# Seven experts' results through a table in device memory, fetched per token, in place of spreading matmuls

## The reference, cut to what matters

```python
def moe_swiglu(h, w_router, w1, w3, w2):
    logits = (h @ w_router).astype(jnp.float32)
    top_val, top_idx = lax.top_k(logits, TOP_K)          # TOP_K = 2
    probs = jax.nn.softmax(top_val, axis=-1)
    combine = jnp.sum(jax.nn.one_hot(top_idx, N_EXPERTS, dtype=jnp.float32) * probs[..., None], axis=-2)
    combine = combine.astype(h.dtype)
    out = jnp.zeros_like(h)
    for e in range(N_EXPERTS):
        out = out + combine[..., e:e + 1] * swiglu(h, w1[e], w3[e], w2[e])
    return out
```

## Time and profile before

| | us |
|---|---|
| runs, median (lowest to highest) | 2058.24 (2054.41 to 2058.87) |
| the profiled execution's own time | 2054.22 |
| its span, first to last instruction | 2052.4 |
| PE busy | 2012.1 (98%) |
| VectorE busy | 1580.0 (77%) |
| ScalarE busy | 1247.0 (61%) |
| POOL busy | 13.9 (1%) |
| HBM read; written | 513.28 MB; 2.12 MB |

### The profile page before, as it was taken

How to read it: one execution, slowest core, us unless ns; L and a number is a source line. 1 busy time by engine, 2 the same in 40 slices (tenths; PEclk the granted TensorE clock), 3 DMA queues, 4 the chain that set the end, 5 groups by cost and what they waited for, 6 DMA issues and landing times.

```text
span 2052.4 us, 28693 instructions
## 1 busy us (share of the span) xinstructions
PE 2012.1 (98%) x10737; PEld 1722.1 (84%) x10737; DVE 1580.0 (77%) x1218; ACT 1247.0 (61%) x1060; POOL 13.9 (1%) x21
## 2 busy tenths in 40 slices
PE   9999999999999999999989999999999999999998
PEld 8988888789998987888878888888888888888887
DVE  5778855755445878865768898888989889898987
ACT  5655455443334664455447777777777777777775
POOL 0000000000000000000000000000000000000000
PEclk9999999999999999999999999999999999999999
DMA  8523455255554523455249999999999999999996
GB/s 277 167 80 106 143 182 184 83 184 185 184 184 146 183 83 103 144 172 182 98 154 329 378 364 380 370 358 377 358 382 353 380 369 357 377 358 381 354 374 243
DMA packets 240765, 516.53 MB, mean 252 GB/s; under 512 B 11528, under 2 KB 34312, under 8 KB 240686
## 3 DMA queue, kind: packets, MB, share of 16 engines
q1 hardware_dynamic: 238274, 507.33, 69.9%
q0 software_dynamic: 2144, 7.88, 1.1%
q10 hardware_dynamic: 268, 0.22, 0.0%
HBM read 513.28 MB, written 2.12 MB: 251 GB/s over the span
## 4 chain that ended last, share of the span: by engine, by line
PE 92%; DVE 4%; issue 2%; ACT 2%; DVEq 0%; ACTq 0%
PE PS L476 27%; PE PS L478 27%; PE PS L477 27%; PE PS L560 7%; PE PS L1063 1%; ACT hi L1186 1%; PE PS L1026 1%; PE PS L780 1%; PE PS L694 0%; PE PS L811 0%; DVE t_n L1704 0%; PE PS L1014 0%; DVE b_gc L2014 0%; PE PS L493 0%; PE PS L649 0%
## 5 line engine op out<-in xcount | busy, mean ns | idle before, releaser
L1681 DVE TENSOR_TENSOR lo<-raw,hi 128x2048 fp32r<-128x2048 f32 x481 | 1095.8, 2290 | 289.9 <-ACT hi L1186 287.6
L1186 ACT ACTIVATE hi<-raw 128x2048 fp32r<-128x2048 f32 x481 | 919.7, 1915 | 314.1 <-PE PS L478 307.9
L476 PE MATMUL PS<-hi,e_hi 128*128 128x512 f32 x896 | 355.1, 396 | 1.4 <-DVE e_lo L1704 1.4
L478 PE MATMUL PS<-hi,e_lo 128*128 128x512 f32 x896 | 349.5, 390 | 0.0
L477 PE MATMUL PS<-lo,e_hi 128*128 128x512 f32 x896 | 349.0, 389 | 0.0
L476 PE MATMUL PS<-hi,actT_hi 128*128 128x512 f32 x640 | 253.4, 396 | 3.7 <-DVE lo L1681 3.1
L478 PE MATMUL PS<-hi,actT_lo 128*128 128x512 f32 x640 | 249.6, 390 | 0.0
L477 PE MATMUL PS<-lo,actT_hi 128*128 128x512 f32 x640 | 249.2, 389 | 0.0
L476 PE MATMUL PS<-hi,fT_hi 128*128 128x512 f32 x536 | 208.7, 389 | 0.0
L478 PE MATMUL PS<-hi,fT_lo 128*128 128x512 f32 x536 | 208.7, 389 | 0.0
L477 PE MATMUL PS<-lo,fT_hi 128*128 128x512 f32 x536 | 208.6, 389 | 0.0
(11 more groups left out here) (329 smaller groups left out, 2112.0 us busy)
## 6 DMA issues: line engine op xcount, KB each, us to landing
raw<-in_moe_w SPq DMA_DIRECT2D x336, 1024.0 KB, 5.3
raw<-in_w_in SPq DMA_DIRECT2D x92, 1024.0 KB, 5.1
raw<-in_ffn_w SPq DMA_DIRECT2D x33, 1024.0 KB, 5.2
raw<-in_w_br SPq DMA_DIRECT2D x12, 1024.0 KB, 5.0
raw<-in_w_out SPq DMA_DIRECT2D x8, 1024.0 KB, 5.1
bias<-hankel_dram POOLq DMA_DIRECT2D x1, 1536.0 KB, 12.7
x<-in_x SPq DMA_DIRECT2D x2, 512.0 KB, 5.5
f_gain<-in_norm_ffn POOLq DMA_DIRECT2D x2, 512.0 KB, 3.8
```

What stands on the lines that cost most here:

```text
L476: pe.matmul(out, a_hi, b_hi, start=first, stop=False, skip_group_check=True)
L478: return pe.matmul(out, a_lo, b_hi, start=False, stop=last, skip_group_check=True)
L1186: act.activation(hi[prog.u % SPLIT][:, :], raw[slot][:, :], COPY).then_inc(hi_made.sem, 1)
L1681: dve.tensor_tensor(lo[prog.u % RAW][:, :], raw[prog.u % RAW][:, :], hi[s][:, :].bitcast(F32), ALU.subtract).then_inc(lo_made.sem, 1)
```

## The change: what it does

- The result of expert 0 to 6 is copied by ScalarE (`results_out`) to a float32 tile `y_out` (it has to wait until the write before it has landed) and written by POOL to rows n*128 to n*128+127 of a table `y_dram` in device memory (512 KB each). Rows 896 to 1023 are written once with zeros.
- `scatter` (line 1026), `results` on VectorE (`y_lo`), `add_to_x` (line 2235) and the two transposes of `pick` with their copy are left out of the first turn, except for the last expert, which keeps its spreading at the end. TensorE's wait for VectorE's read of x's sum before `down` becomes a wait for `y_hi_made`, the copy of ScalarE.
- VectorE computes once, in expert 0 (`places`), which table row each token's first and second choice stands in (the zero row where the choice is expert 7 or was not held).
- In expert 7, POOL waits until all seven results have landed and then fetches four tiles of 128 rows x 1024 by indirect DMAs (two token tiles by two choices) into `y_back`, 16 KB per partition; VectorE adds each to x with its weight (`add_back`), one in each of steps 3 to 5, for which the loop is written out, and one before `results_last`.

```diff
@@ -265,9 +266,13 @@
     xT = sb("xT", [P, TT, KT, P], at=bias_at)
     y_hi = sb("y_hi", [P, D], F32R, at=bias_at)
     y_lo = sb("y_lo", [P, D], F32R, at=bias_at + 4096)
+    y_out = sb("y_out", [P, D], at=bias_at + 8192)
+    y_back = sb("y_back", [P, 2 * TT, D])
+    y_at = sb("y_at", [P, 2 * TT], U32)
     PS = ctx.enter_context(nc.psum_tensor("PS", [P, 8, 512], F32))
     fn_dram = nc.dram_tensor("fn_dram", (T, D), F32, kind="Internal").ap()
+    y_dram = nc.dram_tensor("y_dram", (E * P, D), F32, kind="Internal").ap()
...
@@ -1018,8 +1022,8 @@
         def scatter(n):
-            pe.wait_ge(pickT_made.sem, n + 1)
-            pe.wait_ge(y_lo_made.sem, y_lo_made.count(n + 1))
+            pe.wait_ge(pickT_made.sem, n - SPREAD + 1)
+            pe.wait_ge(y_lo_made.sem, y_lo_made.count(n - SPREAD + 1))
             for t in range(TT):
                 for half in range(2):
                     for part, src in enumerate((y_hi, y_lo)):
...
@@ -1093,14 +1097,17 @@
                 down(base - 1, last=True)
             turn_f(base)
             up(0)
-            if not first:
+            if turn and not first:
                 scatter(n - 1)
-            for t in range(TT):
-                ins = pe.transpose(PS[:, 3, t * P:(t + 1) * P], pick[:, t, :], ident)
-            ins.then_inc(pickT_done.sem, 1)
+            if turn or last:
+                for t in range(TT):
+                    ins = pe.transpose(PS[:, 3, t * P:(t + 1) * P], pick[:, t, :], ident)
+                ins.then_inc(pickT_done.sem, 1)
             up(1)
-            if not first:
-                pe.wait_ge(s_read.sem, s_read.count(2 * n - 1))
+            if turn and not first:
+                pe.wait_ge(s_read.sem, s_read.count((n - SPREAD) * 2 - 1))
+            elif not first:
+                pe.wait_ge(y_hi_made.sem, n)
             down(base, first=True)
             turn_f(base + 1)
             step(base + 2)
...
@@ -1574,6 +1581,12 @@
             act.wait_ge(unit_used.sem, used)
             act.activation(y_hi[:, :], bank(4, 5), COPY).then_inc(y_hi_made.sem, 1)
+        def results_out(n, used):
+            act.wait_ge(unit_used.sem, used)
+            act.wait_ge(fn_out.sem, n * 16 + 32)
+            act.activation(y_out[:, :], bank(4, 5), COPY).then_inc(y_hi_made.sem, 1)
         def results_last(turn, used):
             act.wait_ge(y_half.sem, turn + 1)
...
@@ -1597,15 +1610,18 @@
             prep(1)
             silu(base, U + 2 if first else U)
             prep(2 if first else 4)
-            if not first:
+            if not first and turn:
                 results(U + 4)
+            elif not first:
+                results_out(n - 1, U + 4)
             high(base)
             prep(1)
             prep(1)
             silu(base + 1, U + 6)
             prep(1)
-            act.wait_ge(pickT_done.sem, pickT_done.count(n + 1))
-            act.activation(flat(pickT), PS[:, 3, 0:T], COPY).then_inc(pickT_made.sem, 1)
+            if turn or last:
+                act.wait_ge(pickT_done.sem, pickT_done.count(n - SPREAD + 1))
+                act.activation(flat(pickT), PS[:, 3, 0:T], COPY).then_inc(pickT_made.sem, 1)
             prep(3)
             high(base + 1)
             prep(1)
...
@@ -2241,13 +2258,38 @@
...
+        def places():
+            dve.wait_ge(slots_here.sem, 6)
+            pos, base, val, part = (r_t[:, n, :] for n in (14, 16, 17, 18))
+            tt(val, pos, base, ALU.add).then_inc(dve_step.sem, 1)
+            dve.wait_ge(dve_step.sem, prog.step())
+            dve.scalar_tensor_tensor(val, pos, float(P), val, ALU.is_lt, ALU.mult).then_inc(dve_step.sem, 1)
+            dve.wait_ge(dve_step.sem, prog.step())
+            for k in range(2):
+                tt(part, r_t[:, 4 + k, :], val, ALU.mult).then_inc(dve_step.sem, 1)
+                dve.wait_ge(dve_step.sem, prog.step())
+                dve.tensor_reduce(r_t[:, 19, k * TT:(k + 1) * TT], part.rearrange("p (t e) -> p t e", t=TT),
+                                  AX.X, ALU.add).then_inc(dve_step.sem, 1)
+                dve.wait_ge(dve_step.sem, prog.step())
+            dve.tensor_scalar(y_at[:, :], r_t[:, 19, 0:2 * TT], float(SPREAD * P), None, ALU.add).then_inc(row_made.sem, 1)
+        def add_back(c):
+            if c == 0:
+                dve.wait_ge(e_rows_here.sem, 16 * (SPREAD + 2 * TT))
+            t = c % TT
+            dve.scalar_tensor_tensor(x[:, t, :], y_back[:, c, :], r_t[:, 11, c:c + 1], x[:, t, :],
+                                     ALU.mult, ALU.add).then_inc(dve_step.sem, 1)
+            dve.wait_ge(dve_step.sem, prog.step())
...
@@ -2276,17 +2318,19 @@
             prep(2 if first else 3)
             multiply(base, U + (4 if first else 2))
             prep(1 if first else 2)
-            if not first:
+            if turn and not first:
                 results(n - 1)
             low(base)
             prep(1)
             prep(1)
-            if not first:
+            if turn and not first:
                 for t in range(TT):
                     add_to_x(n - 1, e - 1, t)
             prep(2)
             multiply(base + 1, U + 8)
             prep(2)
+            if first and turn == 0:
+                places()
             if not last:
                 choose(n + 1, e + 1, turn)
             low(base + 1)
...
@@ -2298,12 +2342,21 @@
             prep(1)
             if not last and turn == 0:
                 keep_row(n + 1)
-            with prog.loop(dve, STEPS_EXPERT - 4, 0) as i:
-                prep(3)
-                multiply(base + 3 + i, i * 6 + (U + 20))
-                prep(2)
-                low(base + 3 + i)
-                prep(1)
+            if last and turn == 0:
+                for i in range(STEPS_EXPERT - 4):
+                    prep(3)
+                    multiply(base + 3 + i, i * 6 + (U + 20))
+                    prep(2)
+                    low(base + 3 + i)
+                    prep(1)
+                    add_back(i)
...
...
@@ -2445,15 +2500,29 @@
         pool.iota(slots_i[:, 0:TT], pattern=[[P, TT]], base=0, channel_multiplier=1).then_inc(slots_here.sem, 1)
         pool.wait_ge(slots_here.sem, 3)
         pool.tensor_copy(ids[:, :], slots_i[:, 0:TT]).then_inc(slots_here.sem, 1)
+        pool.wait_ge(slots_here.sem, 4)
+        pool.iota(slots_i[:, 0:TT * E], pattern=[[0, TT], [P, E]], base=-SPREAD * P, channel_multiplier=0)\
+            .then_inc(slots_here.sem, 1)
+        pool.wait_ge(slots_here.sem, 5)
+        pool.tensor_copy(r_t[:, 16, :], slots_i[:, 0:TT * E]).then_inc(slots_here.sem, 1)
+        pool.memset(y_out[:, :], 0.0).then_inc(slots_here.sem, 1)
         pool.wait_ge(norm_made.sem, norm_made.at(1, 5))
         pool.dma_start(fn_dram.rearrange("(t p) d -> p t d", p=P), fn[:, :, :]).then_inc(fn_out.sem, 16)
         pool.wait_ge(fn_out.sem, 16)
+        pool.wait_ge(slots_here.sem, 7)
+        pool.dma_start(y_dram[SPREAD * P:E * P, :], y_out[:, :]).then_inc(fn_out.sem, 16)
         for n in range(1, E):
-            pool.wait_ge(row_made.sem, n)
+            pool.wait_ge(row_made.sem, n + 1)
             if n > 1:
                 pool.wait_ge(e_done.sem, e_done.count(2 * n))
             pool.indirect_dma_start(e_rows[:, :], None, fn_dram[:, :],
                                     bass.IndirectOffsetOnAxis(ap=row_i[:, 0:1], axis=0)).then_inc(e_rows_here.sem, 16)
+            pool.wait_ge(y_hi_made.sem, n)
+            pool.dma_start(y_dram[(n - 1) * P:n * P, :], y_out[:, :]).then_inc(fn_out.sem, 16)
+        pool.wait_ge(fn_out.sem, 32 + 16 * SPREAD)
+        for c in range(2 * TT):
+            pool.indirect_dma_start(y_back[:, c, :], None, y_dram[:, :],
+                                    bass.IndirectOffsetOnAxis(ap=y_at[:, c:c + 1], axis=0)).then_inc(e_rows_here.sem, 16)
```

More of the change, by code:

```diff
@@ L68 @@
 PAIRS = E // 2
+SPREAD = E - 1
 K_ID, K_LE, K_GT, K_M0, K_MT, K_N = 0, 1, 2, 3, 4, 11
@@ L1002, in find_rows @@
         def find_rows(n):
-            pe.wait_ge(pickT_made.sem, n)
             pe.wait_ge(pick_made.sem, 2 * n + 2)
@@ L1113, in expert @@
             if not last:
-                if not first:
-                    pe.wait_ge(s_read.sem, s_read.count(2 * n))
+                if turn and not first:
+                    pe.wait_ge(s_read.sem, s_read.count((n - SPREAD) * 2))
                 if turn == 0:
@@ L1133, in experts @@
             if turn:
-                pe.wait_ge(s_read.sem, s_read.count(2 * E * turn))
+                pe.wait_ge(s_read.sem, s_read.count(2))
             n = E * turn
@@ L2211, in choose @@
             dve.wait_ge(e_done.sem, e_done.count(2 * n))
-            dve.wait_ge(pickT_done.sem, pickT_done.count(n))
+            if turn:
+                dve.wait_ge(pickT_done.sem, pickT_done.count(n - SPREAD))
             for t in range(TT):
@@ L2231, in add_to_x @@
         def add_to_x(n, e, t):
-            dve.wait_ge(s_done.sem, 2 * n + t + 1)
+            dve.wait_ge(s_done.sem, (n - SPREAD) * 2 + t + 1)
```

(21 more changed lines are left out.)

## The result

The changed kernel took 2068.47 us (median of 5 runs, 2067.58 to 2069.97), beside 2058.24 us before (5 runs, 2054.41 to 2058.87): ratio 1.0055, 95% interval 1.004 to 1.007. It is slower by 10.2 us. The forecast was 2045, faster by 13, with 2038 to 2053 as its range.

A forecast was written before the change was run, and what follows sets the result against it. The prediction took TensorE, busy 98%, as the bound, with weight DMA nearly as tight. Removed work of 14.6 us less 2.2 us for the burst gave -12.4 us, so 2045 us, range 2038 to 2053.

The forecast's parts named there:

- the removal: TensorE: spreading matmuls and `pick` transposes go in seven experts, 14.6 us saved, all on the path.
- Landing: Weight units: land within 9.0 us behind one write, 10.7 to 13.3 us behind the last expert's four gathers.
- `places` in expert 0: VectorE, expert 0: seven small operations, 1.2 us once, covered by slack, so no cost.
- burst of four gathers: Expert 7: four gathers, 2.1 MB, hold up the weights; TensorE idle 2.2 us, bounds 0 and 8.8.
- three add_backs in steps: VectorE, steps 3 to 5 of expert 7: one add_back of about 1.29 us each, at no cost.
- The period: Experts 1 to 6, gather to gather: 119.0 us instead of 121.08, DMA having room at 379 GB/s.
- 9.8 us bound: Weight units: a landing up to 9.8 us after being asked for costs TensorE nothing.
- in front of the weights: DMA queues: POOL's transfers go first, queue 0 having 96.3% and the weights' queue 3.9% while a gather moves.
- 16.4 still fits: VectorE, steps 3 to 5 of expert 7: 15.1 us of work becomes 16.4 with an add_back, within 16.81.
- (d): Rival, slower: weights already at a DMA ceiling of 369 GB/s, experts take 122.3 us, total 2072; chance 0.05.
- (c): Rival, no change, 2058: ceiling a little below 379 GB/s, or TensorE idle at the down's new wait; chance 0.08.
- (b): Rival, dear burst in expert 7: each small transfer costs weights 2.4 us, total 2052.4 or 2048.4; chance 0.14.

The follow-up runs named there:

- after_pad4: Changed kernel with four waits on a signal given long ago put into TensorE's program ahead of its loop over expert pairs: 2049.23 us, ratio 0.9967.
- flat_best: flat_halves, with ScalarE's `hi` copy also put ahead of `y_out` and `places` computed ahead of expert 0: 2045.8 us, ratio 0.9947 to the kernel before.
- flat_halves: flat_spread, with each add_back also cut into two halves of 512 columns at VectorE's gaps: 2047.62 us, ratio 0.996 to the kernel before.
- flat_spread: Changed kernel with TensorE's pair loop written out, the last expert's gathers seven units apart, each add_back waiting for its own: 2046.31 us, ratio 0.9951.

## Why the prediction was wrong

**The step that failed** is the removal: "7 x 1.86 = 13.0 us, 7 x 0.22 = 1.5 us: 14.6 us (...), all of it on the path". As time that is right. The sum has no term for what the removal does to the code, so it stands at nothing, and 21.1 us were measured. I took instructions for time only. They are also code, and TensorE's loop begins behind them. Four fewer ahead of it (the pair of transposes in expert 0, which I had even counted) put its start at -2, and each of the two jumps back then cost 9.64 and 11.46 us. The trace of before had the hint, queue 8, empty in two turns of the loop: something that could be lost.

The account for the profiled execution, against the span of before (the burst is taken from after_pad4, see **Landing**):

| | forecast, us | measured, us |
|---|---|---|
| spreading and transposes gone | -14.6 | -14.6, less 7 x 0.19 = 1.3 |
| `places` in expert 0 | 0 | +0.6 |
| burst of four gathers | +2.2 | +3.0 |
| three add_backs in steps | 0 | +1.5 |
| two misses | not seen | +21.1 |
| already later ahead of the experts | - | +2.1 |
| sum | -12.4 | +15.0 (span: +15.4) |

**The period.** 119.0 forecast, 119.18 measured, at 379 GB/s: DMA had the room. The 0.19 us have a place. ScalarE now copies `y_out` (1.03 us), `fT_hi`, and only then `hi`, so VectorE gets that `hi` late and one step takes 17.04 instead of 16.81 us. The spreading matmuls had covered it; I had named the order but priced it at nothing. flat_best turned the order round and its periods grew, so that part is argued and not shown.

**places**: two blocks of transposes of expert 0 are 34.47 us apart. Before it was 34.09, less the 0.22 of the transposes 33.87, so 0.6 us are new. I had called it covered.

**Landing.** Units behind the first write landed in up to 8.9 us (up to 9.0 forecast). The slowest of experts 1 to 6 took 9.6 us, still under the 9.8 us bound; in flat_halves one took 10.8 and TensorE lost time. Behind the four gathers it was 9.7 to 12.5 (10.7 to 13.3 forecast). The 3.0 us are from after_pad4, where no miss disturbs: two steps 36.65 us, against 35.74 before less the 2.08 removed. (In the changed kernel itself the two steps took 37.18 us, 3.5 for the burst, by which the account would close at 15.5.) The gathers took POOL not 0.95 but 2.3 to 2.5 us each. And their bytes didn't go in front of the weights, as I had read from the earlier trace rows. The DMA view from 1968 to 1972 us gives queue 0, POOL's, 49.3% and queue 1, the weights', 53.1%. The burst, priced by its bytes, came out near its forecast of 2.2 us all the same.

**add_back.** "16.4 still fits" into 16.81 was a sum over a step, and a sum says nothing of order. The add_back stood between two `lo` subtractions for which TensorE waits, while VectorE's gap lay elsewhere; 3 x 0.49 us. In halves at the gaps it is hidden, as it was forecast.

**Rivals.** None of them was right. The result ends on the side of (d), which had 0.05, but (d) was a DMA ceiling at 369 GB/s, and 379 were held. (c) named the wait at the down: the waits show none. (b) would have been 6 us or more for the burst; it was 3.0.

**Open.** Why misses begin between +62 and +66 and whether -2 to 0 is a border of a piece (no view shows where pieces begin). No place from +129 on was tried, so whether the map repeats with the pieces isn't known. Why a place gives one or two misses, and 2 or 10 us, stays open, and so does the kernel before at exactly -2, which wasn't tried.

## What to carry to other kernels

An edit that adds or removes instructions ahead of a long hardware loop moves the loop's code, and that alone can cost more than the edit is worth: two instructions decided here some 18 us of 2068 (ratios 1.0055 and 0.9967). When a change loses more than its parts explain, compare the periods with and without a jump back, and look for TensorE idle at the jump, often but not always put down to "issue", and for pieces on the instruction queue. A few waits ahead of the loop, or the loop written out, test it in one run. And a sum of busy times that fits into a step doesn't place the work: put added work into the engine's gap, and don't send several gathers off together in front of a stream that others wait for.

## What was not expected of the hardware

- TensorE's instruction queue brings pieces of 16 KB. With its start in a good place a loop of 1810 instructions stays in for all its turns; in a bad one 8 or 9 pieces come again in each turn (changed kernel), nine more over the program for each miss.
- A miss costs 1.7 to 2.0 us with the clock kept, 5.1 to 11.5 with the granted clock at 0.50.
- A wait already met is not free for TensorE in bulk: 126 instructions of them took 8.9 us ahead of the experts and 13.4 at the program's start. Spread through the loop, 96 took nothing.
- POOL needed 2.3 to 2.5 us to issue each of the four gathers from `y_dram`, and 0.98 for each from `fn_dram`. It isn't the table alone: in flat_spread the first gather from `y_dram` took 0.99 us, the other three 1.63 to 2.86.
- Two queues with work share in more than one way: 96.3% for POOL's beside one gather, 49.3 and 53.1% while four gathers were under way.
